# Two-layer hybrid decoder trunk: the second layer's experts in order of load, twelve light ones as six pairs

## The reference, cut to what matters

```python
D_MODEL, SEQ, N_EXPERT_GROUPS, EXPERTS_PER_GROUP, EXPERT_TOPK = 1024, 256, 4, 8, 2
D_EXPERT = D_MODEL // 4                                  # 256; 32 experts in all

g_w, g_sel = lax.top_k(softmax(t @ w_group), 1)          # one group of eight a token
e_val, e_sel = lax.top_k(e_logits_of_that_group, 2)      # two experts in it
e_w = softmax(e_val) * g_w
for e in range(32):
    he = silu(t @ w_gate[e]) * (t @ w_up[e])
    y = y + combine[:, e, None] * (he @ w_down[e])
```

## Time and profile before

| | us |
|---|---|
| median of three runs | 692.44 |
| span of the profiled execution | 690.7 |
| what lies around the span, against the median | 1.7 |
| start of the second layer's experts on TensorE | 475.7 |
| TensorE's last matmul | 683.05 |
| PE busy | 651.0 (94%) |
| bytes moved | 273.31 MB, mean 396 GB/s |

### The profile page before, as it was taken

The page is one execution under the profiler, slowest core; times in us unless marked ns, Lnnn a source line. Parts: engine busy times, 40 slices in busy tenths (PEclk is TensorE's granted clock), DMA queues, the critical chain, the costliest instruction groups (busy, mean ns, idle before and its releaser), DMA issues.

```text
span 690.7 us, 13056 instructions
## 1 busy us (share of the span) xinstructions
PE 651.0 (94%) x4864; PEld 399.9 (58%) x4864; DVE 251.7 (36%) x661; ACT 121.3 (18%) x317; POOL 64.9 (9%) x187
## 2 busy tenths in 40 slices
PE   4889899998899999999999999999999999999995
PEld 1445465554554555557888788877555555555552
DVE  1014423222222223235689495255322232232233
ACT  4013530000000000014234323237000000000003
POOL 7000021101001011100000000001111111011000
PEclk9999999999999999999999999999999999999998
DMA  9999999999999999999997989963999999999981
GB/s 354 418 422 422 427 419 438 428 431 426 431 428 431 433 428 426 423 421 420 417 422 280 417 339 425 422 280 136 419 428 422 425 427 426 421 424 427 423 357 64
DMA packets 27256, 273.31 MB, mean 396 GB/s; under 512 B 3140, under 2 KB 3652, under 8 KB 4936
## 3 DMA queue, kind: packets, MB, share of 16 engines
q1 hardware_dynamic: 27208, 272.65, 94.3%
HBM read 271.59 MB, written 1.05 MB: 395 GB/s over the span
## 4 chain that ended last, share of the span: by engine, by line
PE 86%; DMA 9%; issue 2%; ACT 1%; SPq 1%; DVE 1%; ACTq 0%; DVEq 0%
PE bank L760 77%; DMA ring<-in_ada_w_dram 9%; PE bank L968 8%; PE bank L1361 1%; SPq L468 0%; ACT hx L1849 0%; PE bank L1215 0%; PE bank L1222 0%; DVE ye L1890 0%; ACT reg_b L1653 0%; ACTq L164 0%; DVE ye L1887 0%; SPq L562 0%; DVE keep L1890 0%; ACT reg_b L1698 0%
## 5 line engine op out<-in xcount | busy, mean ns | idle before, releaser
L760 PE MATMUL bank<-ring,xh 128*64 128x256 f32 (+1 forms) x2496 | 332.9, 421 | 13.4 <-issue 12.6
L760 PEld LDWEIGHTS bank<-ring,xh 128*64 128x64 f32 x2496 | 185.1, 137 | 116.5 <-issue 50.5
L714 POOL COPY xh<-reg_a 128x256 f32 (+1 forms) x130 | 51.6, 397 | 451.0 <-PE bank L760 316.9
L1563 ACT ACTIVATE reg_c<-bank 128x128 f32<-128x128 f32 x64 | 17.7, 277 | 390.9 <-PE bank L760 390.9
L1887 DVE TENSOR_TENSOR reg_c<-reg_c,bank 128x128 f32<-128x128 f32 x64 | 18.4, 287 | 178.6 <-ACT reg_c L1563 178.6
L968 PE MATMUL bank<-ye,reg_b 32*128 32x512 f32 (+1 forms) x528 | 64.3, 600 | 0.0
L760 PE MATMUL bank<-reg_b,ring 128*128 128x256 f32 x256 | 57.2, 380 | 0.4 <-ACT reg_b L1698 0.4
L1887 DVE TENSOR_TENSOR ye<-bank,reg_c 128x512 f32<-128x512 f32 (+1 forms) x66 | 44.3, 671 | 32.4 <-PE bank L760 32.0
L2100 DVE COPY xh<-bank 128x128 f32<-128x128 f32 x64 | 18.2, 285 | 96.0 <-PE bank L760 96.0
L760 PEld LDWEIGHTS bank<-reg_b,ring 128*128 128x128 f32 x256 | 48.0, 190 | 7.1 <-issue 0.9
L760 PE MATMUL bank<-ring,cact 128*32 128x512 f32 (+1 forms) x320 | 34.1, 536 | 16.4 <-DMA ring<-in_ada_w_dram 16.1
(11 more groups left out here) (183 smaller groups left out, 402.2 us busy)
## 6 DMA issues: line engine op xcount, KB each, us to landing
ring<-in_exp_w_dram SPq DMA_DIRECT2D x41, 2048.0 KB, 17.3
ring<-in_exp_w_dram SPq DMA_DIRECT2D x20, 3072.0 KB, 16.0
ring<-in_ada_w_dram SPq DMA_DIRECT2D x48, 1024.0 KB, 17.7
ring<-in_exp_w_dram SPq DMA_DIRECT2D x44, 1024.0 KB, 18.3
ring<-in_w_qkv_dram SPq DMA_DIRECT2D x12, 1024.0 KB, 16.2
ring<-in_w_o_dram SPq DMA_DIRECT2D x4, 1024.0 KB, 8.7
gu_spare<-in_exp_w_dram SPq DMA_DIRECT2D x1, 2048.0 KB, 20.2
hx<-in_exp_w_dram SPq DMA_DIRECT2D x2, 1024.0 KB, 19.7
```

The source lines that it names most:

```text
L714: nc.gpsimd.tensor_copy(xe[:, b, k0:k1, t * CAP:(t + 1) * CAP], hS[:, k0:k1, bass.ds(off, CAP)])\
L760: return nc.tensor.matmul(o_, l_, r_, start=start, stop=stop)
L1563: nc.scalar.activation(sil[:, b, :], bank[b][:, 0:P], ACT.Silu).then_inc(S("sil_ready", L), 1)
```

## The change

The first seven experts (0 to 6) keep their places, so that they can be fetched before the routing is known. The 25 others are put into places 7 to 31 on the chip (`order_experts`, VectorE): those with more than 16 tokens in a tile first, those with at most 16 in both tiles last. SyncE reads the expert of each place from `order_i` before it issues. TensorE's work is cut into 26 units (`UNITS`) instead of 32: places 0 to 18 singly, in the order 0, 1, 2, 3, 7, 8, 9, **4**, 10, 11, 12, **5**, 13, 14, 15, **6**, 16, 17, 18; places 19 to 30 as six pairs; place 31 alone. The three places outside the ring are now 4, 5 and 6. In a pair each expert has 16 slots per tile, so 32 columns, and its four products (two experts, gate and up's two halves) lie side by side in the array's four column strips of 32. From unit 14 (`LATE`) on TensorE works in sequence: rows of u-2, turn of u-1, down of u-1, hidden of u.

```diff
-ALONE = ({R: R}, {10: R, 17: FREED, 24: SPARE})
+ALONE = ({R: R}, {4: R, 5: FREED, 6: SPARE})
...
+LIT = E - 1 - 2 * NLP
+LIGHTS = [(LIT + 2 * n, LIT + 2 * n + 1) for n in range(NLP)]
+UNITS = [(p,) for p in (0, 1, 2, 3, 7, 8, 9, 4, 10, 11, 12, 5, 13, 14, 15, 6, 16, 17, 18)] + LIGHTS + [(E - 1,)]
+NU = len(UNITS)
+LATE = NU - 12
...
+            sp.wait_ge(S("off_ready"), 3)
+            e = expert_of(STAT)
+            gate_up(1, e, *exp_at(1, STAT))
+            for p in range(STAT, E):
+                if p + 1 < E:
+                    following = expert_of(p + 1)
+                    gate_up(1, following, *exp_at(1, p + 1))
+                down_part(1, e, *exp_at(1, p))
+                e = following
+                if p == STAT + 1:
                     sp.wait_ge(S("tab_full"), 2)
                     sp.wait_ge(S("ovf_ready"), 2)
                     down_part(1, last, SPARE, 0)
-            sp.wait_ge(S("dn_ready", 1), early + 1)
+            sp.wait_ge(S("dn_ready", 1), UNITS.index((early,)) + 1)
...
+            def hidden_unit(u, b):
+
+                pe.wait_ge(S("xe_ready", 1), u * 2 + 3)
+                w = []
+                for p in UNITS[u]:
+                    s, fill = loaded(1, p)
+                    w.append(gate_up_w(s).rearrange("p (g k j f) -> p k j g f", g=2, k=KC, j=2))
+                    pe.wait_ge(S("ring_first", s), fill)
+                    pe.wait_ge(S("ring_mid", s), fill)
+                pe.wait_ge(S("heT_ready", 1), u - 1)
+                waited()
+                if len(w) == 1:
+                    last = hidden(bank[b][:, 0:F], lambda k, j: w[0][:, k, j, :, :], b)
+                else:
+                    for k in range(KC):
+                        for x in range(2):
+                            for j in range(2):
+                                g = CAP * (2 * x + j)
+                                last = mm(bank[b][g:g + CAP, 0:F], xe[:, b, k, x * CAP:(x + 1) * CAP], w[x][:, k, j, :, :],
+                                          k == 0, k == KC - 1)
+                last.then_inc(S("gu_ready", 1), 1)
+
...
+                pe.wait_ge(S("ye_ready", 1), u + 1)
+                waited()
+                for t in range(T):
+                    for half in range(2):
+                        rows = slice(64 * half, 64 * half + 64)
+                        last = nc.tensor.matmul(bank[4 + half + 2 * t][:, :], share_light[rows, b, t, :], ye[rows, b, :],
+                                                start=False, stop=False, skip_group_check=True)
+                last.then_inc(S("rows_added", 1), 1)
+
...
+            def expert_unit(u):
+
+                b = u % 2
+                turn_he_of(1, u - 1, 1 - b)
+                hidden_unit(u, b)
+                down_unit(u - 1, 1 - b, u >= 3)
+                if b:
+                    rows_unit(u - 3, 0)
+                    rows_unit(u - 2, 1)
+
+            def late_unit(u):
+
+                b = u % 2
+                if u > LATE:
+                    rows_unit(u - 2, b)
+                turn_he_of(1, u - 1, 1 - b)
+                if u == LATE:
+                    rows_unit(u - 2, b)
+                down_unit(u - 1, 1 - b, True)
+                hidden_unit(u, b)
+                if u == NU - 1:
+                    rows_unit(u - 1, 1 - b)
+                    turn_he_of(1, u, b)
...
+            def table_light(t):
+
+                return mm(bank[2 + t][:, :], ones[:, :], diag[:, t, :, :].rearrange("p f q -> p (f q)"), True, True)
...
+            def expert_unit(u):
+
+                if u >= LATE:
+                    free_downs(u - 1)
+                act.wait_ge(S("gu_ready", 1), u + 1)
+                for s in slots_of(u):
+                    act.sem_inc(S("ring_free", s), 1)
+                nc.scalar.activation(sil[:, u % 2, :], bank[u % 2][:, 0:P], ACT.Silu).then_inc(S("sil_ready", 1), 1)
+                if u == NU - 1:
+                    load_table(ACT.Sqrt)
+                if u == 0:
+                    take_table(1)
+                elif u < LATE:
+                    free_downs(u - 1)
...
+                if L:
+                    nc.vector.memset(hS[:, :, NSLOT:PAD], 0.0).then_inc(S("hS_pad"), 1)
+                    order_experts()
...
+                if L:
+                    take_gathered(L)
...
-                nc.vector.memset(hS[:, :, NSLOT:PAD], 0.0).then_inc(S("hS_pad"), 1)
+                if L == 0:
+                    nc.vector.memset(hS[:, :, NSLOT:PAD], 0.0).then_inc(S("hS_pad"), 1)
+                    take_gathered(L)
+                else:
+                    places_by_rows()
...
+            def order_experts():
+
+                free = slice(STAT, E)
+                nc.vector.tensor_scalar(place_of, of_expert, 1.0 / RANKS, None, ALU.mult)
+                then(nc.vector.tensor_scalar(fits, cnt[:, E + STAT:2 * E], float(LIGHT), None, ALU.is_le))
+                then(stt(fits, cnt[:, free], float(LIGHT), fits, ALU.is_le, ALU.mult))
+                then(nc.vector.tensor_tensor_scan(fit_n, ones[:, 0:ND], fits, 0.0, ALU.mult, ALU.add))
+                then(stt(others, place_of[:, free], 0.0, fit_n, ALU.add, ALU.subtract))
+                then(stt(moved, fit_n, E - 1.0, others, ALU.add, ALU.subtract))
+                then(nc.vector.tensor_scalar(moved, moved, fit_n[:, ND - 1:ND], None, ALU.subtract))
+                then(tt(moved, moved, fits, ALU.mult))
+                then(tt(place_of[:, free], others, moved, ALU.add))
+                then(nc.vector.tensor_scalar(chosen, place_of[0:E, :], own_part[0:E, :], None, ALU.is_equal))
+                tt(of_place[:, 0, :], chosen, of_expert[0:E, :], ALU.mult)
+                then(tt(of_place[:, 1:3, :], offc[0:E, :].rearrange("p (t n) -> p t n", t=T),
+                        chosen.unsqueeze(1).broadcast_to([E, T, E]), ALU.mult))
+                then(nc.vector.tensor_reduce(of_place_sum, of_place, AX, ALU.add))
+                tt(order_diag, ident[0:E, 0:E].unsqueeze(1).broadcast_to([E, 3, E]),
+                   of_place_sum.unsqueeze(2).broadcast_to([E, 3, E]), ALU.mult).then_inc(S("diag_ready"), 1)
+
...
+            def places_by_rows():
+
+                dve.wait_ge(S("counts"), 3)
+                then(nc.vector.tensor_scalar(order_f[0:1, :], order_at[0:1, 0:E], 1.0 / RANKS, None, ALU.mult))
+                nc.vector.tensor_copy(order_i[:, :], order_f[0:1, :]).then_inc(S("off_ready"), 1)
+                nc.vector.tensor_copy(off_at, order_at[0:1, E:3 * E]).then_inc(S("off_ready"), 1)
...
+            def late_unit(u):
+
+                take_heT(1, u - 1, 1 - u % 2)
+                for v in range(u - 1 - (u == LATE), u):
+                    match_unit(v)
+                    dve.wait_ge(S("rows_added", 1), v - 1)
+                    share_unit(v, v % 2)
+                    take_ye(1, v, v % 2)
+                gate_he(1, u, u % 2)
 
```

328 lines of the change are left out of this document (247 added, 81 removed).

## The result

The changed kernel takes 706.64 us (median of 4 runs, 705.45 to 707.84) against 692.49: ratio 1.0204, interval 1.0191 to 1.0217, 14.1 us slower. The forecast was slower, 702.3 us, with a range up to 706.5; the time lies just outside it. The profiled execution took 705.45 us with a span of 703.8, 13.1 us more than before, and all of that stands in the second layer's experts. The runs also lie further apart than before: 2.4 us against 0.2.

A forecast was written before the change was run, and what follows sets the result against it. Transfers and TensorE were both taken to be at their limit, with the last weights' landing deciding. TensorE's end 8.2 us later plus 1.7 for the clock gave 9.9; 692.44 + 9.9 = 702.3 us, range 691.5 to 706.5.

The forecast's parts named there:

- together 10.2 us: Weights' queue in the second layer's experts: dry 3.6 us before place 19 and 6.6 us before place 20.
- so unit 14 is at 572.6: Start of the late sequence: unit 14 through hidden 12.0 us after unit 13 at 560.64, releasing place 19's transfer.
- 7.03 us: Late sequence after unit 14: time per unit, 5.39 + 1.04 + 0.6, putting unit 16 at 586.7.
- I take +0.6; the ends are 0 and 1.2: Start of the stage: hidden of unit 0, and with it the transfers, 0.6 us later through VectorE's added instructions.
- +0.65 us: Start of the stage: table of four records one after another, 1.7 us against 1.07, delaying TensorE but not transfers.
- The last down lands at 682.0: End of the weights' queue: last transfer lands at 682.0 instead of 672.5, after the dry time.
- The 1.7 us: Last pair's down, after 4.4 us idle: TensorE starts at its lower clock and loses 1.7 us; ends 0 and 5.1.
- 2: Rival: not slower, the queue never runs dry, last landing 672.5 + 0.6; 691.8 us; 14%.
- 5: Rival: slower feed of the pairs, by weight loads or a slot 2 us late; 704.5 us; 6%.
- 4: Rival: too few light experts, a pair's expert overflows and waits for its own transfers; 716 us and more; 3%.
- 1: Rival: queue runs dry as forecast, but the clock stays up; 700.6 us; 22%.
- 3: Rival: clock stays at 1.2 GHz to TensorE's end, doubling 11.2 us of late work; 710 us; 7%.

The follow-up runs named there:

- seventh run: Changed kernel plus eight constant matmuls in unit 14's wait and eight more ahead of each down and hidden of a pair; 706.17 us.
- fourth run: Changed kernel with places 4, 5 and 6 worked at units 10, 17 and 21 and the late sequence starting at unit 18; 694.18 us.
- fifth run: Changed kernel with the last unit's hidden multiply ahead of the last pair's down, and its gate ahead of the pair's eviction; 704.52 us.
- sixth run: Changed kernel with eight constant 128x128x128 matmuls in the wait between turn and rows of unit 14; 705.86 us.
- eleventh: The fourth run's kernel with the gathered rows' last two pieces scaled ahead of VectorE's gate arithmetic, its end left as it was; 693.77 us.
- tenth: The ninth's kernel with half the table multiply behind the second unit's hidden and VectorE's table copies behind its gate; 690.44 us.
- ninth: The eighth's kernel with ScalarE's last silu ahead of its slot-freeing wait, and the last unit's turn ahead of the pair's rows; 689.46 us.
- first: Changed kernel with the late sequence starting at unit 18 instead of 14; 702.87 us.
- second: Changed kernel with the down of unit 13 ahead of the rows of unit 12, at unit 14 alone; 704.5 us.
- third: Changed kernel with places 4, 5 and 6 worked at units 10, 17 and 21 instead of 7, 11 and 15; 699.01 us.
- eighth: The fourth run's kernel with the fifth's tail and the gathered rows' last two pieces scaled ahead of VectorE's gate arithmetic; 691.23 us.
- twelfth: The ninth's kernel with eight constant matmuls in each of the two waits around the last but one pair's down; 689.32 us.

## Why the prediction was right and wrong

**What bounds the stage: right.** The count of bytes on the queue gave the sign. Of TensorE's 38.6 us of saved work nothing is seen in the time: between 610 and 680 us it was idle for 20 us and the transfers ran on at 425 GB/s, and a clock held up there won nothing (seventh run).

**The places outside the ring: right in mechanism, and the step that failed in size.** The queue ran dry at the two places named, before place 19 and before place 20, and moving the three places later and the sequence too took 12.5 of the 14.1 us away (fourth run). But the term "together 10.2 us" measured 13.1. It was built with a full clock at unit 14. The fifth run's profile, the same program there at a full clock, has 11.1. So:
- The time of unit 14, "so unit 14 is at 572.6". It was 575.3, 2.7 us later: 0.7 us came with unit 13 (561.33, forecast 560.64), 0.3 us was short in the sum of 12.0 (12.3 at a full clock), and 1.6 to 1.7 us was the clock, which fell to its lower level after one wait of 1.83 us. The wait was forecast, the fall was not. It is worth 1.7 to 2.0 us of lost transfers (13.1 against 11.4 in the sixth run and 11.1 in the fifth). That it fell in the profiled execution, and not in the fifth run's of the same program, was chance.
- The period of "7.03 us". It was 7.3, and the queue behind place 20, which the forecast held for safe, stayed thin: 342 GB/s in 590 to 600 us and 374 in 600 to 610 (place 21 was issued at 597.40 against 593.7, place 22 at 605.07). This, the 0.3 us above and the late start are the remaining 0.9 to 1.2 us; no run separates them.

**The start: wrong in size, "I take +0.6; the ends are 0 and 1.2".** The first issue was 1.19 us late, at the upper end, and the transfers lost 2.3 us by 560 us, beyond it. The forecast shifted one issue. But the next issues wait for the second and third unit, and the four table matmuls (1.99 us, forecast 1.7, before 1.07) stand ahead of them: 7.39 us from the first issue to the third, before 6.49. The +0.65 us had been put down as "for TensorE alone". With a queue that starts empty, TensorE's delays are the transfers' delays. That these 2.3 us come to the end one for one is argued from the bytes and not shown by a run: the eleventh was to show it, and its 0.4 us are within what the runs differ by. The tenth shows that the table's share is not to be had by moving it.

**The sum to the landing.** "The last down lands at 682.0"; it landed at 686.85: 1.7 us from the start, 2.9 from the dry time, 0.25 the rest.

**The end: right in sum, by a chain I had half named.** From the landing to TensorE's end 9.3 us were forecast and 9.25 measured. What set the end, though, was the landing of the last pair's down and 11.5 us of work in series behind it, of which the last unit's hidden need not be there (from the eleventh run to the ninth 4.3 us, with ScalarE's and VectorE's order; about 1.5 us of it is the clock).

**The clock at the end: wrong in the profiled run, and that hid a part of the miss.** The 1.7 us were not paid there: the wait before the last pair's down was 0.98 us instead of the forecast 4.4, and the clock, low in the hidden multiply before it, was back at 681 us. The Trainium skill (TensorE: Matmul & The Clock Gate, HAM oscillation) says that bursts shorter than the waits start each at the lower clock. The traces agree in part. Here the waits are shorter than the burst of hidden, rows and turn (6 us), and the clock falls in some of them all the same: of the fifth run's pairs one had its hidden in 3.66 us, at 1.00, behind a wait of 1.54 us, and the next in 5.77 us, low, behind one of 1.29 that followed on a wait of 3.86. The last down and hidden took 7.0 to 7.9 us behind waits of 1.97 to 3.82 us (first, second, third, fourth, sixth and eleventh run) and 5.53 behind 0.98 and 1.34 (the changed kernel and the seventh run); with hidden first, behind at most 1.22 us, 5.5 us (fifth, eighth, ninth, tenth and twelfth). So a price of 1.5 to 2.4 us was about rightly forecast for a wait that the profiled execution didn't have. This chance and that at unit 14 are good candidates for the spread of 2.4 us, but the sixth and seventh run did not end the spread, and the profiled execution, the fastest of the four, has the lowest mean clock of them (0.969; the others 0.971 to 0.976). So its cause is open.

So 702.3 - 1.7 (clock) + 4.85 (landing) is 705.45, the profiled execution's own time; the median of the runs lies 1.2 us above it, where I had forecast none. Two opposite errors stand in this sum: that it ends only 3.2 us off in the profiled execution is in part luck, the landing alone is off by 4.85.

**The rivals.** 2 (the queue never dry) and 5 (slower feed of the pairs: 64 records of hidden took 3.66 us at a full clock, as much as 32 of a single unit) are out by the trace. 4 (an overflow) is out: such an item fetches weights of its own, and the bytes moved are the same (273.32 MB, before 273.31). 1 had the clock at the end right for the profiled execution and 3 had it wrong (1.00 from 681 us on); both had the same wrong landing. What I had not thought of is that a low clock at one place upstream frees a ring slot late and so goes through a dry queue to the end, and the range was built with the clock at the tail only.

Left open: what the pairs are worth by themselves. The ninth kernel has them and is 3 us faster than before, but a version of it without pairs was not run; nor was the kernel before with the ninth's order at its end.

## What to carry to other kernels

Where a queue of transfers and TensorE are both near their limit, count a change in bytes: write down for each slot which unit frees it and when the queue gets there, and look first at the slots that another order moves. A unit that frees no ring slot costs least where the queue is long or where nothing more waits for a slot; here moving three of them from units 7, 11 and 15 to 10, 17 and 21 gave 7.6 us, and no other placing was run. At the end of a stage, list the work in series behind the last two or three landings, on all engines; a semaphore wait that another engine does first for housekeeping (here to free a slot) can stand ahead of the one instruction that everything waits for.

## What the runs showed of the hardware

- One wait of 1.83 us for VectorE, after a long stretch without a pause, stands in ten of the profiles where nothing fills it. Behind it the granted clock fell to 0.50 for some 3 us in five (the changed kernel, the fourth, ninth, eleventh and twelfth run) and stayed at 1.00 in five (first, third, fifth, eighth and tenth). It fell and stayed in two profiles of the same program up to there (the changed kernel and the fifth run). Each fall cost the unit 1.6 to 1.7 us (14.3 us between two silus instead of 12.6 in the ninth and tenth run).
- Eight matmuls on constants in its place took 2.05 us, and the clock was 1.00 in both profiles with them; five of ten had that without them.
- The 48 records of the last down and hidden took 5.5 us behind waits of up to 1.34 us (seven profiles) and 7.0 to 7.9 us behind waits of 1.97 to 3.82 us (six profiles). Inside the pairs it is less regular: 16 records of a down took 1.92 us, at a full clock, behind a wait of 3.51 us in the fifth run, and 3.64 behind one of 3.86.
- Products of 32 columns, four side by side, cost a pair no more than a single expert: 3.66 us for the 64 records of 128x32 against 3.65 for 32 of 128x64.
- From fastest to slowest the changed kernel's runs lie 2.4 us apart (4 runs), those of the ninth run 0.7 (5 runs), those of the kernel before 0.2 in the first set of 4 and up to 1.3 in a set of 13. What makes the spread isn't shown.
